# Expert weights fetched two units at a time, another order of requests, and three edits around the router

## What is computed

```python
def hier_moe(h, w_group, b_group, w_expert, b_expert, w_gate, w_up, w_down):
    # gates: (tokens, 32), two non-zero entries a row, from a top-1 group and its top-2 experts
    def expert(acc, prm):
        wg, wu, wd, gt = prm
        hid = jax.nn.silu(h @ wg) * (h @ wu)
        return acc + gt[:, None] * (hid @ wd), None
    out, _ = lax.scan(expert, jnp.zeros_like(h), (w_gate, w_up, w_down, gates.T))
```

## Time and profile before

| what | value |
|---|---|
| three timed executions, median | 647.74 us |
| the three | 647.32, 647.74, 649.65 us |
| the profiled execution, its own time | 650.56 us |
| its span, first to last instruction | 648.8 us |
| PE busy | 613.0 us (94%) |
| DVE, ACT, POOL busy | 172.9, 143.4, 71.3 us |
| read from HBM | 247.26 MB, mean 383 GB/s over the span |
| mean granted TensorE clock | 0.991 of full speed |

### The profile page before, as it was taken

One profiled execution on the slowest core, in us unless ns is written; L12 is line 12 of the kernel. 1 busy time (PEld: TensorE's weight loads), 2 busy tenths in 40 slices (PEclk: granted clock), 3 DMA queues, 4 the chain that ended last, 5 costly groups with the idle time before them and its releaser, 6 DMA issues.

```text
span 648.8 us, 8732 instructions
## 1 busy us (share of the span) xinstructions
PE 613.0 (94%) x3465; PEld 321.7 (50%) x3465; DVE 172.9 (27%) x318; ACT 143.4 (22%) x335; POOL 71.3 (11%) x159
## 2 busy tenths in 40 slices
PE   5999999999969999999999899999999999998993
PEld 5886587544754453544535354453544535344331
DVE  3734477970662110102101010210101101020104
ACT  4111334350632121211212121121211212122122
POOL 4800040020132110101101010110101101000000
PEclk9999999999979999999999999999999999999998
DMA  8999998699838999999999999999999999999991
GB/s 315 366 364 352 412 401 315 245 422 421 326 131 320 380 423 422 420 420 422 422 423 421 421 422 422 422 422 420 422 420 422 424 422 420 422 420 421 421 380 69
DMA packets 45324, 248.72 MB, mean 383 GB/s; under 512 B 5377, under 2 KB 5453, under 8 KB 19181
## 3 DMA queue, kind: packets, MB, share of 16 engines
q1 hardware_dynamic: 42880, 244.33, 92.7%
q0 software_dynamic: 944, 2.79, 1.2%
q10 hardware_dynamic: 1470, 1.22, 0.6%
HBM read 247.26 MB, written 1.07 MB: 383 GB/s over the span
## 4 chain that ended last, share of the span: by engine, by line
PE 65%; DMA 22%; issue 7%; DVE 2%; POOL 1%; SPq 0%; ACT 0%; DVEq 0%; ACTq 0%; POOLq 0%
PE PS L1651 28%; DMA W<-in_w_up_dram 16%; PE PS L1666 12%; PE PS L1576 6%; PE PS L1289 5%; DMA W<-in_w_in_dram 4%; PE PS L1618 3%; DMA W<-in_w_ada_dram 3%; PE PS L1460 2%; PE PS L1586 2%; PE PS L1499 1%; PE PS L1680 1%; PE PS L1242 1%; DVE rt L1068 1%; PE PS L1256 1%
## 5 line engine op out<-in xcount | busy, mean ns | idle before, releaser
L1651 PE MATMUL PS<-W,XT 128*64 128x512 f32 x832 | 200.1, 595 | 7.9 <-DMA W<-in_w_up_dram 7.5
L1651 PEld LDWEIGHTS PS<-W,XT 128*64 128x64 f32 x832 | 63.9, 137 | 109.5 <-issue 107.0
L1158 DVE TENSOR_SCALAR XT<-PS,scol,shcol 128x128 f32<-128x128 f32 x64 | 21.9, 404 | 235.5 <-PE PS L1576 235.5
L1666 PE MATMUL PS<-V,HT 128*64 128x512 f32 x256 | 56.7, 595 | 1.5 <-DVE XT L1158 1.5
L1141 DVE SCALAR_TENSOR_TENSOR YL<-PS,gcol,YH 128x1024 fp32r<-128x1024 f32 x15 | 19.3, 1284 | 134.5 <-ACT YH L778 134.5
L1576 PEld LDWEIGHTS PS<-OH,H 128*128 128x128 bf16 x768 | 45.7, 116 | 12.4 <-issue 12.4
L1666 PE MATMUL PS<-W,HT 128*64 128x512 f32 x224 | 49.6, 595 | 0.0
L1576 PE MATMUL PS<-OH,H 128*128 128x128 bf16 x768 | 48.2, 225 | 0.0
L870 DVE SCALAR_TENSOR_TENSOR MOD<-W,cS,MOD 128x2048 f32<-128x2048 f32 x16 | 37.6, 2348 | 11.7 <-DMA W<-in_w_ada_dram 11.3
L778 ACT ACTIVATE YH<-PS,gcol 128x1024 fp32r<-128x1024 f32 x15 | 16.7, 1113 | 98.5 <-PE PS L1666 98.5
L1666 PEld LDWEIGHTS PS<-V,HT 128*64 128x64 f32 x256 | 18.2, 137 | 35.6 <-issue 35.6
(11 more groups left out here) (236 smaller groups left out, 592.3 us busy)
## 6 DMA issues: line engine op xcount, KB each, us to landing
W<-in_w_up_dram SPq DMA_DIRECT2D x62, 1024.0 KB, 18.2
W<-in_w_gate_dram SPq DMA_DIRECT2D x40, 1024.0 KB, 20.1
V<-in_w_down_dram SPq DMA_DIRECT2D x32, 1024.0 KB, 18.7
W<-in_w_down_dram SPq DMA_DIRECT2D x30, 1024.0 KB, 19.8
W<-in_w_ada_dram SPq DMA_DIRECT2D x16, 1024.0 KB, 8.1
V<-in_w_gate_dram SPq DMA_DIRECT2D x16, 1024.0 KB, 22.5
W<-in_w_in_dram SPq DMA_DIRECT2D x12, 1024.0 KB, 7.6
W<-in_w_ada_dram SPq DMA_DIRECT2D x16, 512.0 KB, 5.5
```

The source lines that it names most:

```text
L1158: nc.vector.tensor_scalar(XT[:, k, :], PS[:, 3, (k - 4) * P:(k - 3) * P], scol2[:, k:k + 1], shcol2[:, k:k + 1], ALU.mult, ALU.add).then_i ...
L1651: last = nc.tensor.matmul(PS[rows, u // 2, :], XT[:, k, rows], home(odd, unit_of(u, which), p)[:, q * FF:(q + 1) * FF], start=(k == 0), st ...
L1666: last = nc.tensor.matmul(PS[rows, 2 + q % 2, :], HT[:, k, rows], home(odd, unit_of(u, which), p)[:, q * FF:(q + 1) * FF], start=(k == 0), ...
```

## The change

**The layout.** A partition now holds neighbouring rows of the whole matrix: 8 rows of gate or up, 4 of down (16 KB in HBM), of which a unit takes the first or the second half. All strided reads follow: gather and transpose_x2 read every eighth column, turn_over_half every fourth; both column groups of X are needed for a transpose, so `transpose_x2(2)` waits for x2_ready 3. The router's weights come in two requests, not four. The strips become 64 rows in two banks, ACT copies 64 x 1024, and turn_strips does eight transposes in place of four.

**Requests of 2 MB.** In turns 2 to 13 (`JOINED`) units v and v + 2 that live side by side (`TAIL_OF`: 0/2, 4/6, 5/7, 8/10, 9/11; not 0/2 in odd turns) are fetched by one request of 128 partitions x 16 KB, asked for at the place and under the wait of the second. Both count as landed together. An even turn has 5 such requests and 2 single units, an odd turn 4 and 4: 54 in all.

**The order of requests.** From outer turn 2 to 6 the list is `SINGLES_FIRST` = 3, 4, 5, 6, 7, then 0, 1, 2, 8 to 11.

**The router.** POOL makes the third part of the first block alone, DVE that of the second, right behind m16; POOL's G2 waits for `placed`. DVE's L1049 and ACT's L759 stand one or two steps earlier. PE's filler products before the places are 24, not 9.

The third part of the second block (L1141) came between. The core of the diff:

```diff
+SINGLES_FIRST = tuple(v for v in range(UPT) if v not in TWO_HOMES) + TWO_HOMES
+TAIL_OF = {0: 2, 4: 6, 5: 7, 8: 10, 9: 11}
+JOINED = range(2, TURNS - 2)
...
-                v = w.rearrange("l e (h p k) f -> h (l e) p (k f)", p=P, h=2)[u % 2]
+                v = w.rearrange("l e (p h k) f -> h (l e) p (k f)", p=P, h=2)[u % 2]
...
+            def fetch_two(v, odd, e):
+                tile = VP[v] if in_own(odd, v, 0) else WP[v]
+                sp.dma_start(tile[:], two_units_source(e, v // 2)).then_inc(landing(odd, v, 0), 16)
...
             def load_unit(turn, v):
                 user = turn - (2 if v in TWO_HOMES else 1)
+                if joined(turn, v) and v in TAIL_OF:
+                    return
                 sp.wait_ge(unit_used[v % 2], UPE * user + v // 2 + 1)
-                fetch(v, turn % 2, 2 * turn + v % 2)
+                if joined(turn, v):
+                    fetch_two(v - 2, turn % 2, 2 * turn + v % 2)
+                else:
+                    fetch(v, turn % 2, 2 * turn + v % 2)
...
                 for turn in range(1, RUN_AHEAD + 1):
-                    for v in range(UPT):
+                    for v in range(UPT) if turn == 1 else SINGLES_FIRST:
                         load_unit(turn + 1 if v in TWO_HOMES else turn, v)
...
-            for t in range(TT):
-                pool.wait_ge(mid_ready, t + 1)
-                nc.gpsimd.tensor_tensor(H3[:, 2, t, :], Hn[:, t, :], H3[:, 1, t, :], ALU.subtract).then_inc(h3_ready, 1)
+            pool.wait_ge(mid_ready, 1)
+            nc.gpsimd.tensor_tensor(H3[:, 2, 0, :], Hn[:, 0, :], H3[:, 1, 0, :], ALU.subtract).then_inc(h3_ready, 1)
             pool.wait_ge(mod_row, 2)
+            pool.wait_ge(placed, 1)
             nc.gpsimd.tensor_tensor(G2[:], G2[:], GU[:], ALU.mult).then_inc(gained, 1)
...
             nc.vector.tensor_tensor(m16[:], o1, o2, ALU.add).then_inc(routed, 1)
+            dve.wait_ge(mid_ready, 2)
+            nc.vector.tensor_tensor(H3[:, 2, 1, :], Hn[:, 1, :], H3[:, 1, 1, :], ALU.subtract).then_inc(h3_ready, 1)
...
-            turn_over(9, 1)
+            turn_over(24, 1)
...
-                        first = k // 4 * FF + k % 4
                         for t in range(TT):
                             for part in range(3):
-                                last = nc.tensor.matmul(PS[:, 2 + k // 4, k % 4 * P:(k % 4 + 1) * P], H3[:, part, t, first:first + FF - 3:4],
+                                last = nc.tensor.matmul(PS[:, 2 + k // 4, k % 4 * P:(k % 4 + 1) * P], H3[:, part, t, k:k + D - 7:8],
```

More of the change, by code:

```diff
@@ L106, in sem @@
             return ctx.enter_context(nc.semaphore(name))
-        W = [sb(f"W{slot}", [P, UW]) for slot in range(RING)]
+        WP = {v: sb(f"WP{v}", [P, 2 * UW]) for v in TAIL_OF}
+        W = [None] * RING
+        for head, tail in TAIL_OF.items():
+            W[slot_of(BASE + head)] = WP[head][:, 0:UW]
+            W[slot_of(BASE + tail)] = WP[head][:, UW:2 * UW]
+        for v in (1, 3):
+            W[slot_of(BASE + v)] = sb(f"WS{v}", [P, UW])[:]
         X = sb("X", [P, TT, D])
@@ L316, in landing, with joined, landings @@
             return own_in[v] if in_own(odd, v, p) else unit_in[slot_of(BASE + v)]
-        def unit_arrived(eng, i, odd, v, p):
-            if in_own(odd, v, p):
-                eng.wait_ge(own_in[v], i * 16 + 16)
-            elif p == 0 and v in TWO_HOMES:
-                eng.wait_ge(unit_in[slot_of(BASE + v)], i * 16 + 16 * uses_of(BASE + v))
-            else:
-                fills = uses_of(BASE + v) + odd + TURNS * p - (TURNS // 2 if v in TWO_HOMES else 0)
-                eng.wait_ge(unit_in[slot_of(BASE + v)], i * 32 + 16 * fills)
+        def joined(turn, v):
+            return turn in JOINED and any(v in pair for pair in TAIL_OF.items()) and not (turn % 2 and v in ODD_OWN)
+        def landings(turn, v):
+            tails = tuple(TAIL_OF.values())
+            return sum(in_own(t % 2, v, 0) == in_own(turn % 2, v, 0) and not (v in tails and joined(t, v))
+                       for t in range(turn + 1))
+        def unit_arrived(eng, i, odd, v, p):
+            if p:
+                first = uses_of(BASE + v) - 1 + max(landings(TURNS - 2 + t, v) for t in range(2) if not in_own(t, v, 0))
+                eng.wait_ge(unit_in[slot_of(BASE + v)], i * 32 + 16 * (first + TURNS * (p - 1) + odd + 1))
+                return
+            before = 0 if in_own(odd, v, 0) else uses_of(BASE + v) - 1
+            if isinstance(i, int):
+                eng.wait_ge(landing(odd, v, 0), 16 * (before + landings(2 * i + odd, v)))
+                return
+            if joined(2 + odd, v) and v not in TAIL_OF:
+                v -= 2
+                before = 0 if in_own(odd, v, 0) else uses_of(BASE + v) - 1
+            first, step = landings(2 + odd, v), landings(4 + odd, v) - landings(2 + odd, v)
+            eng.wait_ge(landing(odd, v, 0), i * (16 * step) + 16 * (before + first - step))
         def halves_arrived(eng, u, q, p):
@@ L1412, in turn_strips @@
                 pe.wait_ge(strips_out, 1)
-                for q in range(4):
-                    last = nc.tensor.transpose(PS[:, 4, q * P:(q + 1) * P], modR[:, q:q + HALF - 3:4], ident[:])
+                for k in range(DC):
+                    last = nc.tensor.transpose(PS[:, 4, k * 64:(k + 1) * 64], modR[:, k:k + D - 7:8], ident[0:64, 0:64])
                 last.then_inc(mod_turned, 1)
```

60 lines of the change are left out of this document (32 added, 28 removed).

## The result

| what | before | changed |
|---|---|---|
| median of 20 executions, us | 648.88 | 650.97 |
| least and most, us | 645.03, 650.79 | 649.39, 657.13 |
| the profiled execution, us | 650.56 | 651.51 |
| its span, us | 648.8 | 649.7 |
| mean granted TensorE clock in it | 0.991 | 0.995 |

The forecast was 644.7 us, 3.0 us faster than before; the time lies above the range of 641.0 to 650.5 by 0.5 us. 1.1 us of the 6.3 between forecast and result is the median of before itself, which was 647.74 from three executions and is 648.88 from twenty; the other 5.1 are errors of terms.

The account below looks back on a forecast made before the run. The DMA request stream was taken to bound the kernel, PE losing 9.4 us to data. Terms -3.5 + 4.8 + 1.7 - 6.0 = -3.0 us took the 647.74 us median to 644.7 us, range 641.0 to 650.5.

Parts of the forecast that it names:

- no hole follows: Refill stream after 39.6 us from the first refill request: releases outpace the work done, so no later loss was charged.
- the rate: DMA stream: 16 KB packets save 0.116 us a pair, 52 pairs ahead of the deciding unit, 6.0 us earlier (0.7 to 8.7).
- router and clock: Before turn 0: places start 2.05 us earlier, gather takes 2.80 us instead of 5.10; together 4.35 us earlier.
- order and waiting for pairs: Early refills: the queue runs dry behind waiting pairs, 4.8 us later; pairs landing together in turn 13, 1.7 us later.
- SINGLES_FIRST alone changes who waits, not the stream's length: Request order: up units of turns 5 and 6 come three units earlier, but the end gains nothing; charged at nothing.
- pairs landing together: Turn 13: all four up units must be there before u = 2, where two sufficed; 1.7 us later (0 to 1.7).
- Strips: Before turn 0: two column groups instead of four and four more transposes cost 0.1 to 1.2 us, taken as 0.8.
- Strides: Gather's stationary operand: going from a step of 8 bytes to 16 was charged nothing, from float transposes loading equally fast.
- rival B: The gather slows to 5.10 us, 2.3 us more each, deciding from 0.66 us a gather: 671.6 us; chance 0.06.
- A: DMA requests: 16 KB rows are cut, so only completions are saved, 0.7 us; +2.3 us, 650.0 us; chance 0.12.
- D: Better than the sum: packets at 18.7 ns and the waiting for pairs hidden, 640.3 us; chance 0.05.
- C: Pairs let the queue run dry in later turns too; three turns with a hole of 1.5 us: 649.2 us; chance 0.07.

Follow-up runs that it names:

- The five kernels: Before plus router's edits, 644.49 us; plus layout and strips, 646.40; plus singles first, 648.09; plus waiting, as two 1 MB requests, 654.79; plus 2 MB requests, 650.97.
- the run with two requests: Changed kernel with each pair asked for at the same place and wait, but as two requests of 1 MB with 8 KB rows: 654.79 us, ratio 1.0098.
- single requests: Changed kernel with every request again one unit of 1 MB (`JOINED` empty), its singles-first order kept: 648.09 us, ratio 1.0005.
- the kernel with both holes filled: Changed kernel with turn 2's pairs requested unit by unit in old order up to there, and turn 8's two-home units ahead of v 3 to 7: 647.89 us.

## Why the prediction was wrong

Two steps of the prediction failed that matter most. "From then on each release adds work faster than it is done, and no hole follows" charged nothing for the later turns, where 2.4 us are lost at 400 us; and the rate, taken as 6.0 us earlier, gave 3.7. The strips and the gather's stride add 1.1. The five kernels set each term beside its measurement, by the medians, by the ratios, and by the profiled executions from the start of the strips to u = 3 of turn 14 (450.77 us before, 452.85 in the changed kernel):

| step | predicted us | medians | ratios | within the span |
|---|---|---|---|---|
| router and clock | -4.35 | -4.3 | -4.5 | -4.8 |
| strips and strides | +0.8 | +1.9 | +2.3 | +1.5 |
| order and waiting for pairs (4.8 + 1.7) | +6.5 | +8.2 | +8.5 | +9.6 |
| rate | -6.0 | -3.7 | -3.3 | -4.2 |
| sum | -3.0 | +2.1 | +3.0 | +2.1 |

The order stands with the waiting, since the 4.8 us were counted with v 0 to 2 behind pair 4/6, as the new order has them; apart they are 1.5 and 6.7 us by the medians. Each measured step is a difference of two results whose ratios to before are each good to 1.0 to 1.8 us, so it is good to about 2 us; the sum is better known, and no step rests on its difference alone.

- **Router: right,** in its size and its places. m16 was 0.8 us later than told, with L1090 beside POOL's step, but the filler covered it. It is the only term that came out as priced. That gate_up started where it was forecast was luck, though: 0.7 us of it came from the early start of that execution, against 0.6 more for the strips and 0.3 for the gather than were charged.
- **The rate: right mechanism, wrong size.** Queue 1 from 240 to 390 us (packets, MB, share of 16 engines), in before and then in the changed kernel:

```profile
q1 hardware_dynamic: 8677, 63.18, 101.2%
```

```profile
q1 hardware_dynamic: 5534, 63.92, 100.7%
```

Two equations, as in the prediction: 8677 p + 63.18 b = 1.012 x 2400 and 5534 p + 63.92 b = 1.007 x 2400 give p = 12.5 ns a packet, where it said 13.0, and 35,104 packets in all came where it said 35,100. The failed step is "0.116 at a share of 1.01": it turned saved engine time into saved wall time at the share of before. The share fell with it, from 101.2 to 100.7%, so the rate rose from 421 to 426 and not to 428 to 430. 144 units at 2.49 us are 359 us, and 1.2% of that is 4.2; the run with two requests gave 3.7. The bounds of 0.7 to 8.7 held it. Before's row also agrees with the Trainium skill, "DMA: Bandwidth & Descriptors", The descriptor swizzle, on a 1 MB transfer to 128 partitions having nine write descriptors, one of them the completion, on each of 16 engines: 8677 packets in 60.25 units of 1,048,576 bytes are 144.0 a unit.
- **The order: "SINGLES_FIRST alone changes who waits, not the stream's length" is wrong.** It does change it, since free homes then stand behind occupied ones: 1.8 us from 220 to 230 with single requests. And it is not separable: with up pairs the old order is 3.1 us worse. This mistake did little to the sum, whose 4.8 us already hold those units back.
- **"No hole follows": wrong, by 2.4 us.** The early part of the waiting was priced well. Queue 1 in the first 46.4 us behind the first refill request, in before and then in the changed kernel:

```profile
q1 hardware_dynamic: 2496, 18.24, 97.3%
```

```profile
q1 hardware_dynamic: 1621, 16.35, 89.9%
```

1.89 MB less, 4.5 us, where 4.8 were charged relative to before. The order's share is in both. The 2.4 us at 400 us were not foreseen: where the loop of turns ahead ends, the units with two homes are asked for in their own turn again, behind the up pairs. What pairs landing together cost (1.7 charged) was in no run by itself and stays open: of the 8.2 us by the medians, 4.5 and 2.4 leave 1.3, and the 31.8 us from u = 2 of turn 13 to u = 3 of turn 14 are 2.3 over the 29.5 between its starts in turns 6 and 7, where data set the pace, which allows up to that.
- **Strips: mis-sized,** 1.4 against 0.8, above the bounds of 0.1 to 1.2. The products took 1.92 us, 0.85 more, and the transposes 0.45 more, both at the upper ends as told; the failed step is that 0.8 was taken between them.
- **Strides: the failed step is the charge of nothing.** The float loads of the earlier trace rows were no evidence for bf16. 148 ns a load against 113, 0.32 us a gather, half of the 0.66 from which rival B would decide. By the sentence cited from the Trainium skill, "Advanced Engine Details and Errata", SBUF Cachelines, the step should cost, and it does; the 5.10 us of rival B were the lower clock's and far too high.
- **The rivals.** A and B did not happen, nor did D. C named the right mechanism, a queue that runs dry in later turns, and put it at three holes of 1.5 us with a chance of 0.07; the list of requests had evidence for more, since every up pair of turns 2 to 13 waits for u = 3 of the turn before, with free units behind it in the list. With every term as measured the sum is +2.1, as it must be, since each kernel adds one part to the last; what supports the single terms is their own rows.

## What to carry to other kernels

A larger request is asked for when its last part is free, so it moves a wait in front of everything behind it in the list: look in the queue for what stands behind it and has long been free, at every place where the order changes its pattern, not only at the first. Take larger requests where homes come free together anyway (here gate and down units from turn 3 on: 644.13 us), and leave single those that are freed last and needed first (the up units). Even so, count what their layout costs: the router's edits alone, with the old layout, reach 644.49. And price saved DMA work in wall time from a rate, not from engine time: about two thirds of it arrived.

## What the hardware showed that was not expected

**The clock after a wait of 2 us.** Three profiled executions have PE at the lower level after a wait for an up pair. Parts u = 2 in PE's timeline of the kernel with two requests (start us, us, line, operation, idle before):

```profile
365.59 3.65 PE L1692 MATMUL PS<-WP,XT 128*64 128x512 f32 x16 [2.19 <-DMA WP<-in_w_up_dram]
...
395.42 5.35 PE L1692 MATMUL PS<-WP,XT 128*64 128x512 f32 x16 [2.25 <-DMA WP<-in_w_up_dram]
```

The same of the kernel with both holes filled, and a stretch of it, columns as in the earlier trace rows:

```profile
561.03 5.35 PE L1700 MATMUL PS<-WP,XT 128*64 128x512 f32 x16 [1.98 <-DMA WP<-in_w_up_dram]
```

```profile
563.00:565.00 2.00, 2.00 (x6) 0.61 (x4) 0.00 (x0) 0.00 (x0) 0.00 (x0) 0.50 0.98 418
```

The clock is 0.50 of full, the lower level, and the part takes 5.35 us and not 3.65: 1.7 us. It fell after waits of 2.25 and 1.98 us here (and of 2.14 and 2.17 in the changed kernel with the gather at 8 bytes), and not after waits of 2.19, 2.26 and 2.57 in the kernel with two requests, so the length of the wait does not decide alone. In 20 executions of the changed kernel the two with the lowest mean clock, 0.982, were the two longest, 656.54 and 657.13 us; that the waits for pairs cause that was not tried. The eleven executions with 0.992 or more lie between 649.39 and 651.51 us, the other nine between 650.57 and 657.13.

**A step of 16 bytes in bf16.** The 128 x 128 stationary operand of the gather loads in 142 to 171 ns, against 110 to 152 at 8 bytes, and a product follows the next 6 to 7 ns later (0.32 us in 48), though float loads with the same step of 16 bytes were as quick as with 8.

**Where an execution starts from.** The strips started between 140.6 and 142.7 us in these profiled executions, though next to nothing ahead of them differs between the kernels. So one execution's time says little where a microsecond matters; the terms above come from medians, or from differences within a span.
